# Summing the squares of the input on TensorE instead of GpSimd in a two-layer decoder trunk

## What is computed

```python
def rms_norm(x, g):
    xf = x.astype(jnp.float32)
    y = xf * lax.rsqrt(jnp.mean(xf * xf, axis=-1, keepdims=True) + EPS)
    return (y * g.astype(jnp.float32)).astype(x.dtype)

for layer in range(DEPTH):
    if layer % 2 == 0:
        h = h + even_mixer(rms_norm(h, ln_mix_even[i]), w_in_even[i], s5_lambda_re[i], ...)
    else:
        h = h + mla_mixer(rms_norm(h, ln_mix_odd[i]), ...)
    h = h + conv_ffn(rms_norm(h, ln_ffn[layer]), ...)
return rms_norm(h, ln_final)
```

```python
dt = jnp.exp(log_dt.astype(f32))[:, None]
mag = jnp.exp(lr * dt)
ab_re, ab_im = mag * jnp.cos(li * dt), mag * jnp.sin(li * dt)
den = lr * lr + li * li
f_re = (nr * lr + ni * li) / den
bb_re = f_re[..., None] * br - f_im[..., None] * bi
```

## Time and profile before

| | |
|---|---|
| median of three runs | 2346.82 us (2345.45 to 2347.09) |
| the profiled execution | 2346.18 us |
| its span, first to last instruction | 2344.4 us |
| TensorE busy | 2236.5 us (95%) |
| VectorE, ScalarE, GpSimd busy | 64%, 43%, 32% |
| mean granted TensorE clock | 0.98 |

### The profile page before, as it was taken

One profiled execution on the slowest core, in us unless ns is written; L12 is line 12 of the kernel. 1 busy time (PEld: TensorE's weight loads), 2 busy tenths in 40 slices (PEclk: granted clock), 3 DMA queues, 4 the chain that ended last, 5 costly groups with the idle time before them and its releaser, 6 DMA issues.

```text
span 2344.4 us, 47346 instructions
## 1 busy us (share of the span) xinstructions
PE 2236.5 (95%) x18398; PEld 2194.1 (94%) x18398; DVE 1507.4 (64%) x1744; ACT 1002.5 (43%) x1244; POOL 745.1 (32%) x889
## 2 busy tenths in 40 slices
PE   7598888999999999999999999999999999999997
PEld 7587777999999999999999988999999999999997
DVE  7378777577666655666666656677666555666666
ACT  4233333444444444444444445444444444444442
POOL 5789995023333200332311000023323101333211
PEclk9899999999999999999999999999999999999998
DMA  6333333455544456445456433455545556555453
GB/s 252 108 131 113 126 134 113 160 199 192 187 179 179 159 196 219 180 179 179 169 185 207 175 108 116 144 197 177 187 182 181 166 193 212 186 186 181 156 191 120
DMA packets 64460, 398.69 MB, mean 170 GB/s; under 512 B 7153, under 2 KB 9713, under 8 KB 28785
## 3 DMA queue, kind: packets, MB, share of 16 engines
q1 hardware_dynamic: 60048, 391.15, 47.7%
q10 hardware_dynamic: 4320, 6.27, 0.8%
HBM read 395.29 MB, written 2.10 MB: 170 GB/s over the span
## 4 chain that ended last, share of the span: by engine, by line
PE 81%; POOLq 8%; POOL 5%; issue 3%; DVE 2%; ACT 0%; DVEq 0%; ACTq 0%
PE PS L1393 25%; PE PS L1394 25%; PE PS L1397 25%; POOLq L1280 2%; POOLq L1284 2%; POOL g L1282 2%; POOL E L1285 2%; POOLq L1152 2%; POOLq L1159 1%; PE PS L1388 1%; POOL S L1297 1%; PE PS L1389 1%; PE PS L1390 1%; POOLq L1298 1%; PE PS L1734 1%
## 5 line engine op out<-in xcount | busy, mean ns | idle before, releaser
L695 DVE TENSOR_TENSOR lo<-raw,hi 128x1024 fp32r<-128x1024 f32 (+2 forms) x826 | 979.7, 1205 | 571.5 <-ACT hi L350 568.1
L350 ACT ACTIVATE hi<-raw 128x1024 fp32r<-128x1024 f32 (+2 forms) x826 | 785.3, 968 | 791.3 <-PE PS L1397 743.6
L1393 PE MATMUL PS<-XS,hi 128*128 128x256 f32 x3584 | 891.3, 286 | 15.9 <-ACT hi L350 15.9
L1394 PE MATMUL PS<-XS,hi 128*128 128x256 f32 x3584 | 885.0, 284 | 0.0
L1393 PEld LDWEIGHTS PS<-XS,hi 128*128 128x128 f32 x3584 | 692.9, 193 | 24.0 <-issue 15.7
L1394 PEld LDWEIGHTS PS<-XS,hi 128*128 128x128 f32 x3584 | 693.0, 193 | 0.3
L1397 PE MATMUL PS<-XS,lo 128*128 128x256 f32 x3584 | 503.7, 283 | 0.0
L1397 PEld LDWEIGHTS PS<-XS,lo 128*128 128x128 f32 x3584 | 463.1, 192 | 0.0
L1394 PE MATMUL PS<-YF,hi 128*128 128x256 f32 x1408 | 331.9, 276 | 0.0
L1393 PE MATMUL PS<-YF,hi 128*128 128x256 f32 x1408 | 331.8, 276 | 0.0
L1350 POOL TENSOR_TENSOR ctmp<-apad,cws 128x512 f32<-128x512 f32 x88 | 134.8, 1553 | 552.6 <-DVE apad L746 552.6
(11 more groups left out here) (236 smaller groups left out, 2529.8 us busy)
## 6 DMA issues: line engine op xcount, KB each, us to landing
raw<-in_ffn_up SPq DMA_DIRECT2D x176, 1024.0 KB, 4.8
raw<-in_ffn_dn SPq DMA_DIRECT2D x128, 704.0 KB, 4.1
raw<-in_w_in SPq DMA_DIRECT2D x52, 1024.0 KB, 4.8
raw<-in_w_oe SPq DMA_DIRECT2D x16, 1024.0 KB, 4.8
raw<-in_w_oo SPq DMA_DIRECT2D x16, 1024.0 KB, 4.8
raw<-in_mla_dn SPq DMA_DIRECT2D x9, 1024.0 KB, 4.9
raw<-in_w_ukv SPq DMA_DIRECT2D x8, 1024.0 KB, 4.8
raw<-in_w_uq SPq DMA_DIRECT2D x8, 768.0 KB, 4.4
```

The costliest lines, as they stand in the source:

```text
L350: act.activation(hi[:, p % SLOTS, 0:n], raw[:, u % SLOTS, off:off + n], ACT.Copy).then_inc(hi_ready, 1)
L695: V.tensor_tensor(lo[:, p % SLOTS, 0:n], raw[:, u % SLOTS, off:off + n], f(hi[:, p % SLOTS, 0:n]), ALU.subtract).then_inc(lo_ready, 1)
L1393: mm(PS[:, bank, 0:T], wh, x[:, 0:T], start=first, stop=False)
L1394: mm(PS[:, bank, 0:T], wh, x[:, T:2 * T], start=False, stop=False)
```

## The change

GpSimd no longer adds the squares. TensorE sums them instead: after each of the four pieces of the first step x_squares(c) waits for the squares of chunk c and multiplies its four tiles of 256 columns by the matrix of ones, accumulating 16 matmuls in all in bank 7. The first three groups set sq_added, which lets ScalarE reuse the buffer; the last one sets sum_done. The matmuls of norm_sum(0) go. GpSimd's program now starts with line 1321 and the setup, and waits for sum_done before the setup writes into the buffers of the squares.

```diff
-            G.memset(acc[:, :, :], 0.0)
-            for c in range(4):
-                for i in range(2):
-                    pool.drain()
-                    if i == 0:
-                        pool.wait_ge(sq_ready, c + 1)
-                    ins = G.tensor_tensor(acc[:, :, :], acc[:, :, :], (sT1, sT2)[c % 2][:, i], ALU.add)
-                ins.then_inc(sq_added, 1)
...
                 pool.wait_ge(even_loads, 48)
+                pool.wait_ge(sum_done, 1)
...
             def norm_sum(n):
 
-                if n:
-                    pe.wait_ge(ssq_ready, n)
-                else:
-                    pe.wait_ge(sq_added, 4)
+                pe.wait_ge(ssq_ready, n)
...
+            def x_squares(c):
+
+                pe.wait_ge(sq_ready, c + 1)
+                for k in range(4):
+                    ins = mm(PS[:, 7, 0:T], ones[:, :], (sT1, sT2)[c % 2][:, k // 2, k % 2, :], start=c == 0 and k == 0,
+                             stop=c == 3 and k == 3)
+                ins.then_inc(sq_added if c < 3 else sum_done, 1)
...
-            step(0, 0, XSk, before=x_split(0), after=lambda i: norm_sum(0) if i == 3 else None)
+            step(0, 0, XSk, before=x_split(0), after=x_squares)
```

## The result

| | before | after |
|---|---|---|
| median | 2346.38 us (4 runs) | 2332.34 us (4 runs) |
| the profiled execution, its span | 2346.18, 2344.4 us | 2332.27, 2330.5 us |
| transposes of line 1466 (after: 1462) start | 119.25 | 104.22 |
| TensorE's wait for them | 28.3 us | 17.2 us |
| end of the last rotation (GpSimd's memset of line 1125 starts) | 388.98 | 375.12 |

The ratio is 0.9939 with the interval 0.9924 to 0.9955: faster by 14.0 us. 2332.9 had been forecast. Lines from 1136 on have other numbers in the changed kernel: the transposes are 1462, the last instruction of the setup 1259, a chunk's lines 1299 and 1300 are 1290 and 1291, the product with C (1496) is 1492, x_squares is 1437, and the three matmuls of a product are 1384, 1385 and 1388.

The account below looks back on a forecast made before the run. GpSimd's setup, on which TensorE waits 28.3 us, was taken to bound the kernel; 11.8 us from its earlier start plus 2.1 us from TensorE's front gave 13.9 us, 2332.9 us against the median, range 2325.0 to 2338.5.

Parts of the forecast that it names:

- The bound: TensorE waits 28.3 us at the transposes for GpSimd's setup; the time changes by as much as the setup's end moves.
- The start of the setup: GpSimd's setup, freed of the additions, starts at about 10.4 instead of 32.0 us; bounds 10.3 and 12.6.
- The pace: GpSimd's setup beside VectorE before 29.95 us: 0.62 us an instruction, 31.5 instructions, worth 11.8 us; bounds 0.376 and 0.85.
- Rival 2: GpSimd's setup: only VectorE's two-SBUF-input instructions hold it up, eleven costing 5.5 us; 16.2 us gained, 2330.6; chance 0.12.
- TensorE's front: TensorE's first step with the squares: the next step starts at 30.7 instead of 32.83 us, 2.1 us earlier.
- The sum at the transposes: End of GpSimd's setup, line 1466: 13.9 us earlier, at about 105.3, with some 16.5 us of wait left.
- From there on: State-space chunks and after: unchanged, with periods of 68.4 us and the same 1948 us after the state-space part.
- What was costed at nothing: GpSimd's moved wait for sum_done behind even_loads, and ScalarE's square of chunk 2 waiting for TensorE: both cost nothing.
- Rival 1: GpSimd's setup before 32 us is hardly disturbed: 0.376 us an instruction, 19.6 + 2.1 us gained, 2325.1; chance 0.1.
- Rival 3: TensorE's front: squares cause the half clock or get in the way, front 9.7 us late; 9.3 us gained, 2337.5; chance 0.1.
- Rival 5: Transposes of line 1466: something taken for hidden holds them near 119, no gain, 2346.8; chance 0.04.
- Rival 4: State-space chunks lose what the setup gains; with 5 us more a chunk the time would be 2353; chance 0.04.

Follow-up runs that it names:

- the PSUM kernels: Changed kernel with VectorE filling the low parts of pieces 1 to 5, or 1 to 15, from zeros in PSUM: 2328.56 us and 2320.52 us.
- the one-input low parts: Changed kernel with VectorE making the low parts of pieces 1 to 5 from one SBUF input (raw times 1.0): 2333.78 us, ratio 0.9935.
- the early start: Changed kernel with only GpSimd's wait for VectorE's reciprocal moved to its first use in the setup: 2329.74 us, ratio 0.9916.
- the squarings behind: Changed kernel with only the seven squarings of the phasors (35 GpSimd instructions) moved behind the end of the setup: 2333.36 us, ratio 0.9940.

## Why the prediction was right, step by step

- **The bound.** Right. The transposes' end sets the rest: 15.0 us at the transposes, 13.9 at the state-space end, 13.9 in the profiled execution. Putting the additions back took all of it.
- **The start of the setup.** 10.4 forecast, 10.52 measured. The two slow instructions of VectorE (lines 773 and 776) took 0.17 and 0.18 us without the additions, and 1.26 and 1.25 again with the additions put back.
- **The pace.** 0.62 us an instruction was taken from the stretch 32 to 60; it was 0.66 (18.6 us by 28 instructions). 31.5 instructions were forecast by the end of the front, 28 were done. Of TensorE's wait 11.8 us were to go, 11.1 went (28.3 to 17.2); 28 instructions at 0.376 us are 10.5 of them, and in the stretch behind the front, 58.1 us in both kernels, GpSimd did 107 instead of 104. The number was good, the reason given for it only half: the five splits each cost GpSimd 0.8 to 0.96 us (the PSUM kernels), so a count of VectorE's instructions by kind is the better way than a busy share. Rival 2 had that mechanism, but a flat 0.5 us for each instruction and nothing for the scalings, and came out 2 us too fast.
- **TensorE's front.** 2.1 us earlier forecast, 3.9 measured (28.92 instead of 30.7). Piece 0 ended 0.3 us sooner than forecast; the squares behind it took 1.5 us and not 2.1, from 13.59 to the second piece at 15.13; and the three chunks after it took 4.60 us each instead of 4.7, with nothing more for the clock, where 0.6 us had been allowed. An added matmul of squares does cost 0.43 us and not 0.39, but a piece costs 2.88 and not 3.1.
- **The sum at the transposes** was low: 13.9 forecast, 15.0 measured (11.1 + 3.9). The split into these two terms is bookkeeping and not two causes: what TensorE's front gains, GpSimd's new stretch loses, and a front 6.3 us longer moved the transposes by 0.6 to 0.7 us only. Told by cause, the setup starts 21.6 us earlier and loses 6.6 of them on the way, with VectorE's instructions beside it.
- **From there on** the forecast took the rest as rigid, and it isn't quite. 1.1 us of the gain are lost between the transposes and the state-space end. The first rotation's line 1300 had come 30.33 us behind the transposes (149.58), after the change 30.82 (135.04). These 0.5 us are the clock: TensorE starts the transposes at the half clock (granted 0.50), which before ended 3.7 us later and now some 4.6 us later, and the part of the first piece that uses the low parts of the input (line 1397, now 1388) follows the transposes after 5.00 us instead of 4.50. The other 0.6 us go in the chunks: the first line 1299 of a chunk is 14.5 us earlier in the first chunk, 14.3 in the second, 14.0 in the third and 13.9 in the last. What lengthens a period by 0.1 to 0.3 us wasn't tried. So two errors of 1.1 us, one each way, cancelled: the steps were good to about 1 us each, and that the sum is closer than that is chance.
- **What was costed at nothing.** The waits for sum_done, even_loads and sq_added cost nothing: none of them is among the waits of GpSimd or ScalarE in the trace after. The squares on TensorE are hidden up to 17.2 us: doubled they moved the state-space end by about 0.5 us, five times as many were paid beyond 17.2.
- **Slips in the working.** Lines 1299 at 216.43 and 284.86 belong to the first halves of the second and third chunk, not to second halves; the period is the same. The 8.3 us at the slow end of the range don't follow from its terms: with a front that gains nothing and 0.85 us an instruction, 25.5 instructions in 21.65 us give 9.6. And the half pace of piece 0 (0.21 us from record to record, as between 27.4 and 30.8) is not in the granted clock, which reads 1.00 from 8.5 to 13.9; what slowed that piece stays open.
- **The rivals.** Rival 1 (undisturbed) asked for 45 instructions before 29 us; there were 28. Rival 3 (half clock on TensorE) asked for a second step after 33; it came at 28.92, with a granted clock of 1.00. Rival 5 (the end held by something else) falls with the transposes at 104.22. Rival 4 (longer chunks) has 0.6 us of the 20 it asked for: line 1290 of the changed kernel in the timeline of GpSimd, against the earlier trace rows:

```profile
202.15 1.27 POOL L1290 TENSOR_TENSOR S<-S 128x512 f32<-128x512 f32 x1
...
270.82 1.27 POOL L1290 TENSOR_TENSOR S<-S 128x512 f32<-128x512 f32 x1
```

The period is 68.67 us instead of 68.43.

## What to carry to other kernels

When an engine's program is one chain to a wait that ends last, what stands in front of the chain costs what it delays, here 21.6 us for additions of 12 us, because in between they wait for their input. What the earlier start is worth is that shift less what the chain loses beside the work that it now overlaps (here 6.6 us): count the other engine's instructions there by kind, and how long each holds the chain up. And a step moved within such a chain moves its waiters, but gives only the chain's idle time.

## What the runs showed of the hardware

A GpSimd instruction of 0.25 us on 16 columns that falls beside one of VectorE's on 1024 columns lasts about as long as that one when VectorE subtracts two SBUF tensors (1.23 us: 1.22) or multiplies one SBUF tensor (0.76 us: 0.80), and is not held up when VectorE reads PSUM (1.22 us: 0.25). The second case I hadn't expected.

TensorE's pace in a whole stage isn't the same from one execution to another, at the same granted clock (1.00 in the four stretches compared here). In the profile of the kernel with 15 low parts from PSUM each of the two output projections took 3 us longer than in the changed kernel that ran beside it, without a wait (from VectorE's last reciprocal ahead of each to the next one behind it, 99.2 and 99.6 us against 96.2 and 96.6). A group of matmuls in the second one, first of the changed kernel, then of that one (the second number is the mean duration in ns):

```profile
L1388 PE MATMUL PS<-YO,lo 128*128 128x256 f32 x248 | 33.2, 276 | 0.0
```

```profile
L1394 PE MATMUL PS<-YO,lo 128*128 128x256 f32 x248 | 34.3, 281 | 0.0
```

That accounts for 6 of the 6.7 us by which the part behind its state-space end was longer (1961.9 against 1955.2 us), and so for most of what its profiled execution gained less than the state-space end. That its median moved less for the same reason is likely but not shown, for only one of its executions was profiled.

The same two durations stand in the other profiles. The first projection took 99.2 us with the squares five times; the second took 99.6 with the additions put back, the squares twice, the one-input low parts, the early start and the squarings behind; in the rest, the kernel before among them, both took the shorter time. The part behind the state-space end was 1954.1 to 1956.2 us where neither was slow, 1956.9 to 1959.3 where one was, and 1961.9 where both were. So a difference of 3 us between two profiled executions can come from this alone. The four times of the kernel with 5 low parts from PSUM, 2325.96, 2326.24, 2330.88 and 2331.08, lie in two groups; only the first was profiled, so whether this is the same thing isn't shown. What chooses between the two paces stays open.
